# Post-mix and post-FFN norms taken by halves of 288 tokens in an encoder layer

## What is computed

```python
mix = (g_a * (oa @ w_branch_a[i]) + g_b * (ob @ w_branch_b[i])) @ w_out[i]
h = h + rms_norm(mix, g_mix_post[i])
f = jnp.square(jax.nn.relu(rms_norm(h, g_ffn_pre[i]) @ w_up[i])) @ w_down[i]
h = h + rms_norm(f, g_ffn_post[i])
h = h + jax.nn.sigmoid(h @ w_ple_gate[i]) * rms_norm(ple @ w_ple[i], g_ple[i])
```

## Time and profile before

| what | value |
|---|---|
| median of 3 runs | 1178.62 us (1177.7 to 1179.76) |
| the profiled execution | 1179.02 us, span 1177.3 us |
| mean granted TensorE clock | 0.991 |
| TensorE busy | 1151.8 us, 98% of the span |
| VectorE, ScalarE, GpSimd busy | 487.3, 425.9, 508.6 us |

### The profile page before, as it was taken

The page is one execution under the profiler, slowest core; times in us unless marked ns, Lnnn a source line. Parts: engine busy times, 40 slices in busy tenths (PEclk is TensorE's granted clock), DMA queues, the critical chain, the costliest instruction groups (busy, mean ns, idle before and its releaser), DMA issues.

```text
span 1177.3 us, 23187 instructions
## 1 busy us (share of the span) xinstructions
PE 1151.8 (98%) x8374; PEld 1094.8 (93%) x8374; DVE 487.3 (41%) x910; ACT 425.9 (36%) x905; POOL 508.6 (43%) x424
## 2 busy tenths in 40 slices
PE   8999999999999999999999989999999999999897
PEld 7888888888888889999999989999999999999897
DVE  2655555656534341112352276215413421541665
ACT  5344444454443444332233253213212221222342
POOL 3545544453444333333445454534444444444541
PEclk8999999999999999999999999999999999999899
DMA  5233422222232222232222212322222222222122
GB/s 158 82 92 93 137 75 82 89 89 69 84 93 75 92 75 63 81 101 80 81 84 86 63 54 72 99 81 82 87 81 80 80 86 84 80 80 81 53 72 81
DMA packets 167338, 98.82 MB, mean 84 GB/s; under 512 B 8801, under 2 KB 162650, under 8 KB 167282
## 3 DMA queue, kind: packets, MB, share of 16 engines
q1 hardware_dynamic: 159538, 82.05, 24.0%
q0 software_dynamic: 7744, 16.02, 4.2%
HBM read 88.57 MB, written 11.02 MB: 85 GB/s over the span
## 4 chain that ended last, share of the span: by engine, by line
PE 91%; DVE 5%; ACT 1%; issue 1%; POOL 0%; DVEq 0%; ACTq 0%
PE proj L1353 75%; PE turn_out L1525 3%; PE score L1443 3%; PE turn_out L1504 2%; PE turn_out L1520 1%; DVE wide L1219 1%; PE turn_out L1389 1%; PE turn_out L1475 1%; PE score L1450 1%; DVE hT L1248 1%; PE score L1381 1%; ACT prob L679 1%; DVE prob L1043 1%; PE turn_out L1537 1%; DVE act_lo L1237 1%
## 5 line engine op out<-in xcount | busy, mean ns | idle before, releaser
L463 POOL TENSOR_TENSOR w_lo<-w_raw,w_hi 128x512 fp32r<-128x512 f32 x292 | 394.4, 1354 | 587.8 <-ACT w_hi L627 587.6
L1353 PE MATMUL proj<-act_hi,w_hi 128*128 128x288 f32 x1600 | 362.5, 308 | 8.8 <-DVE act_lo L1237 3.5
L1353 PE MATMUL proj<-act_lo,w_hi 128*128 128x288 f32 x1600 | 344.4, 297 | 0.0
L1353 PE MATMUL proj<-act_hi,w_lo 128*128 128x288 f32 x1600 | 343.6, 297 | 0.0
L627 ACT ACTIVATE w_hi<-w_raw 128x512 fp32r<-128x512 f32 x292 | 182.3, 628 | 380.9 <-PE proj L1353 379.2
L1353 PEld LDWEIGHTS proj<-act_hi,w_hi 128*128 128x128 f32 x1600 | 255.0, 190 | 29.8 <-issue 16.6
L1353 PEld LDWEIGHTS proj<-act_lo,w_hi 128*128 128x128 f32 x1600 | 259.0, 190 | 0.0
L1353 PEld LDWEIGHTS proj<-act_hi,w_lo 128*128 128x128 f32 x1600 | 258.8, 190 | 0.0
L1353 PE MATMUL proj<-mid_hi,w_hi 128*128 128x288 f32 x640 | 137.3, 296 | 0.0
L1353 PE MATMUL proj<-mid_hi,w_lo 128*128 128x288 f32 x640 | 137.3, 295 | 0.0
L1353 PE MATMUL proj<-mid_lo,w_hi 128*128 128x288 f32 x640 | 137.3, 295 | 0.0
(11 more groups left out here) (207 smaller groups left out, 1110.7 us busy)
## 6 DMA issues: line engine op xcount, KB each, us to landing
w_raw<-w_in SPq DMA_DIRECT2D x72, 256.0 KB, 3.0
w_raw<-w_up SPq DMA_DIRECT2D x64, 256.0 KB, 2.8
w_raw<-w_down SPq DMA_DIRECT2D x64, 256.0 KB, 2.8
w_raw<-w_gate SPq DMA_DIRECT2D x32, 256.0 KB, 2.7
w_raw<-w_branch_b SPq DMA_DIRECT2D x16, 256.0 KB, 2.9
w_raw<-w_out SPq DMA_DIRECT2D x16, 256.0 KB, 2.8
w_raw<-w_ple_gate SPq DMA_DIRECT2D x16, 256.0 KB, 2.9
out<-k_tm POOLq DMA_DIRECT2D x12, 256.0 KB, 3.8
```

Source lines behind the costliest of these rows:

```text
L463: pool.tensor_tensor(w_lo[:, slot], w_raw[:, slot], w_hi[:, slot].bitcast(F32), ALU.subtract).then_inc(lo_done, 1)
L1353: last = pe.matmul(out[:, h], w[:, slot, at], x[:, k, HALF * h:HALF * h + HALF], start=(k == 0 and s == 0), stop=(k == blocks - 1 and s == 2))
```

## The change

The norms behind `w_out` and behind the last `w_down` group are taken for tokens 0 to 287 and for tokens 288 to 575 apart, each with sums, means, power and row of its own, on 96 partitions by 3 columns.

- TensorE does the last two blocks before the norm half by half: block 6 first half, block 7 first half, block 6 second half, block 7 second half (`last_two`). The sums of the first half stand in the middle of the third of these, its row in the middle of the fourth. The two blocks behind the norm are done for the first half of the tokens over all k, then for the second. Between them and the norm are the four PLE blocks, with the sums of the second half behind the first of them and its row behind the third.
- VectorE, GpSimd and ScalarE do copies, squares, scalings, additions and splits for 288 tokens at a time, first half first. The PLE copies on ScalarE stand between the splits of the first half.
- The pre-FFN norm's sums and row come 4 k-steps later on TensorE than before (`steps_before_sums`), the PLE norm's where they were.
- On ScalarE the eight squares of `ple` stand ahead of the first `gate_ple`.

```diff
-            def behind_norm(half, n, pj, pc):
...
-                project_ple(half, 0)
-                norm_sums(n)
-                project_ple(half, 1)
-                norm_row(n)
-                project_ple(half, 2)
-                project_ple(half, 3)
-                two_tasks(pj, pc, h_split, half * KB)
+            def last_two(n, pj, pc, hi, lo, input_ready):
+                def one(j, h, between):
+                    if h == 0:
+                        wait_projection(Count(pj + j))
+                    for k in range(KB):
+                        p = Count(pc + 2 * j + k // 4)
...
+                        last = half_products(pj + j, p, hi, lo, k, h)
+                        if k == KB // 2 - 1:
+                            between()
...
+                one(0, 0, lambda: None)
+                one(1, 0, lambda: None)
+                one(0, 1, lambda: half_sums(n, 0))
+                one(1, 1, lambda: half_row(n, 0))
             def behind_norm(half, n, pj, pc):
                 project_ple(half, 0)
+                half_sums(n, 1)
                 project_ple(half, 1)
                 project_ple(half, 2)
+                half_row(n, 1)
                 project_ple(half, 3)
+                for h in range(2):
+                    for k in range(KB):
+                        pe.wait_ge(h_split, (2 * half + h) * KB + k + 1)
+                        for j in range(2):
...
+                            half_products(pj + j, p, act_hi, act_lo, k, h)
+            def late_norm(n, pj, pc, steps_before_sums):
                 project(Count(pj + 2), Count(pc + 4), act_hi, act_lo)
-                steps = k_steps(Count(pj + 3), Count(pc + 6), act_hi, act_lo)
-                for _ in range(KB // 2):
+                steps = itertools.chain(k_steps(Count(pj + 3), Count(pc + 6), act_hi, act_lo),
+                                        k_steps(Count(pj + 4), Count(pc + 8), act_hi, act_lo))
+                for k in range(2 * KB):
+                    if k == steps_before_sums:
+                        norm_sums(n)
+                    if k == steps_before_sums + KB // 2:
+                        norm_row(n)
                     next(steps)
...
+            late_norm(N_FPRE, PJ_FF, PC_FF, KB)
...
+            late_norm(N_PLE, PJ_PG, PC_PG, KB // 2)
```

VectorE's update, where `keep` copies a half block out of PSUM and k in BY_VECTOR means the addition is VectorE's:

```diff
+                for k in range(KB - 2, KB):
+                    keep(k, 0)
+                for k in range(KB - 2, KB):
+                    add_square(last_square(2 * n, k, 0), cols=tokens(0))
+                means(2 * n, 0)
+                keep(KB - 2, 1)
+                add_square(last_square(2 * n, KB - 2, 1), cols=tokens(1))
+                dve.wait_ge(row_ready, CHAIN[2 * n] + 1)
+                normed_half(0, 0)
+                normed_half(1, 0)
+                keep(KB - 1, 1)
+                add_square(last_square(2 * n, KB - 1, 1), cols=tokens(1))
+                for k in range(2, KB):
+                    normed_half(k, 0)
+                    rest(k - 2, 0)
+                    if k == 2:
+                        means(2 * n, 1)
+                rest(KB - 2, 0)
+                rest(KB - 1, 0)
+                dve.wait_ge(row_ready, CHAIN[2 * n] + 2)
+                for k in range(KB):
+                    normed_half(k, 1)
+                    if k >= 2:
+                        rest(k - 2, 1)
+                rest(KB - 2, 1)
+                rest(KB - 1, 1)
```

ScalarE, in `next_input` and behind its second call:

```diff
+                for k in range(KB - 2, KB):
+                    square_half(2 * n, x, job, k, 0)
+                for q in range(PC_PLE[n], p):
+                    hi_part(Count(q))
+                square_half(2 * n, x, job, KB - 2, 1)
+                hi_part(Count(p))
+                hi_part(Count(p + 1))
+                square_half(2 * n, x, job, KB - 1, 1)
+                for i in range(KB // 2):
+                    split_hi(i, 0)
+                    keep_ple(n, i)
+                    if i % 2:
+                        hi_part(Count(p + 2 + i // 2))
+                for k in range(KB // 2, KB):
+                    split_hi(k, 0)
+                for k in range(KB):
+                    split_hi(k, 1)
+                    if k >= KB - 2:
+                        hi_part(Count(p + RING + k - (KB - 2)))
...
-            next_input(1, None)
+            next_input(1, down_sum, last_job, None)
+            for k in range(KB):
+                square(SQUARES[N_PLE] + k, ple[:, k])
...
             for m in range(2):
                 gate_ple(m)
                 hi_part(Count(PC_PG + RING + 2 + m))
-            for k in range(KB):
-                square(3 * KB + k, ple[:, k])
```

More of the change, by code:

```diff
@@ L818, in next_input @@
                     else:
-                        act.activation(act_hi[:, k], hT[:, k], ACT.Copy, scale=gcol[:, scale + k:scale + k + 1]
+                        act.activation(act_hi[:, k, c], hT[:, k, c], ACT.Copy, scale=gcol[:, scale + k:scale + k + 1]
                                        ).then_inc(h_hi, 1)
[L822 to L827, removed]
+                for k in range(KB - 2, KB):
+                    square_half(2 * n, x, job, k, 0)
@@ L844, in _ @@
             for k in range(KB):
-                square(KB + k, hT[:, k])
+                square(SQUARES[N_FPRE] + k, hT[:, k])
             for j in range(2, KB):
@@ L1224, in _ @@
+            for m in range(KB - 2):
                 b = (PJ_OUT + m) % 2
@@ L1609, in norm_row, with half_sums @@
             def norm_row(n):
-                pe.wait_ge(r_ready, n + 1)
+                pe.wait_ge(r_ready, CHAIN[n] + 1)
                 row_matmuls(r_t, lambda t: P).then_inc(row_ready, 1)
+            def half_sums(n, h):
+                pe.wait_ge(sq_added, SQUARES[n] + KB + 2 * h)
+                for t in range(3):
+                    first = HALF * h + THIRD * t
+                    last = pe.matmul(turn[0:THIRD, 3 * h + t:3 * h + t + 1], sq_sum[:, first:first + THIRD],
+                                     ones[:, 0:1], start=True, stop=True)
+                last.then_inc(sum_turned, 1)
@@ new lines, in half_row, with half_products @@
+            def half_row(n, h):
+                pe.wait_ge(r_ready, CHAIN[n] + h + 1)
+                for t in range(3):
+                    first = 512 * h + THIRD * t
+                    last = pe.matmul(score[:, first:first + THIRD],
+                                     r_t[0:THIRD, 3 * h + t:3 * h + t + 1].broadcast_to([THIRD, P]),
+                                     ident[0:THIRD, 0:THIRD], start=True, stop=True)
+                last.then_inc(row_ready, 1)
+            def half_products(n, p, hi, lo, k, h):
+                slot, at = p.mod(RING), slice(P * (k % 4), P * (k % 4) + P)
+                for s, (w, x) in enumerate(((w_hi, hi), (w_lo, hi), (w_hi, lo))):
+                    last = pe.matmul(acc[n % 2][:, h], w[:, slot, at], x[:, k, tokens(h)],
+                                     start=(k == 0 and s == 0), stop=(k == KB - 1 and s == 2))
+                if h == 1 and k % 4 == 3:
+                    last.then_inc(w_used, 1)
+                return last
```

239 lines of the change are left out of this document (149 added, 90 removed).

## The result

The changed kernel takes 1182.14 us, median of 15 runs, beside 1178.51 for the kernel before in the same comparison: ratio 1.0031 [1.0024, 1.0039], some 3.7 us slower. The prediction was 1182.7. The profiled execution took 1181.17 us, its span is 1179.6.

The account below looks back on a forecast made before the run. TensorE, busy 98% of the span, loses time waiting for VectorE at two norms. First norm -3.3 + 0.35 + 3.4, second -3.4 + 5.8 + 1.2: +4.05 on 1179.02, 1183.1; median 0.4 lower, 1182.7 us; range 1180 to 1186.

Parts of the forecast that it names:

- VectorE's half chain: First norm: half instructions take 0.45 us; last subtraction ends at u = 26.3, u counted from block 7's old end.
- No wait is there any more: First norm: TensorE reaches the two blocks behind it at u = 10.1, against 15.3, and need not wait.
- the 0.35 that I did count: End of the two blocks behind the first norm: ScalarE's accumulator copy makes TensorE wait 0.35 us more.
- The gains: Stretches around both norms: 3.3 us gained at the first, 3.4 at the second, with VectorE slower than TensorE.
- Given back behind the first norm: Later pre-FFN row returns as waits around the first down block: 1.9 us standing plus 1.5 lower clock, 3.4.
- everything that GpSimd splits there moves with TensorE: Behind the first norm: argument that VectorE's collisions with GpSimd stay, against the later row being absorbed.
- absorbed: Rival, chance 0.18: fewer up-chain collisions with GpSimd remove the later row's 3.4 us; +0.65 left, 1179.3 us.
- Given back behind the second norm: Third gate block: squares ahead of the gate copy make TensorE wait about 5.9 us, then lower clock costs 1.2.
- Costlier halves: Rival, chance 0.10: half instructions on VectorE take 0.53 us, adding 2.9 us in each stretch; 1188.5 us.
- TensorE's pace: Rival, chance 0.12: halves keep pace with TensorE, stretches gain 8.6 and 8.2 us, sum -6.0; 1172.6 us.
- 30.5: First norm: u at which ordinary blocks begin before the change, against 27.2 forecast after it.
- the 3.7 us put to the lower clock: First norm's stretch before the change: 3.7 of 9.0 us lost laid to slow pairs behind two waits.

Follow-up runs that it names:

- the halves' own run: Changed kernel with the PLE squares back behind the second gate copy and the pre-FFN sums and row as early as before: 1172.55 us, ratio 0.9955.
- the run without the additions: Against the halves with squares and pre-FFN row set back: VectorE's six residual additions per norm cut to one column; 1168.98 us, ratio 0.9922.
- filling the gap: Changed kernel plus 42 matmuls with unread results on TensorE before the third gate block: 1179.91 us, ratio 1.0013.
- the whole-block run: Kernel before, whole blocks, with only the eight PLE squares moved ahead of the gate copies: 1181.86 us, ratio 1.0044.

## Why the prediction was right

Point by point, by the prediction's own steps.

- **VectorE's half chain.** A half instruction at 0.45: 0.43 in a chain, as the line of three widths had it. The Trainium skill's page "VectorE: DVE Perf Modes", section on the TRN2 errata, gives 0.457 as an estimate by its formula and advises against such pieces; the rows' 0.43 is near its price, and the halves' own run (0.9955) shows that the advice did not decide here. From the wait-ending addition to the last subtraction I had 22.4 us; it is 22.8 (667.68 to 690.50). Part of that agreement is luck: 36 instructions at 0.43 are 15.5 us where the sum had 16.4, and collisions and waits took some 7.3 where it had 6.0. The addition came at u = 3.6 for 3.9, the wait for the sums was 0.63 for 0.8, VectorE's end u = 26.4 for 26.3.
- **"No wait is there any more" at the two blocks.** One of 0.35 is there, for ScalarE's copy of the last PLE block: the same kind of wait as the 0.35 that I did count at the end of the two blocks. It probably costs nothing by itself, since TensorE catches up with VectorE a few steps on and waits for it there; no run takes it out.
- **The gains**: 3.3 less 0.35 forecast, 2.81 measured; 3.4 forecast, 3.35 measured. The reason given, VectorE as the slower one, is borne out by the waits for `act_lo` and by the run without the additions, in which 2.9 of the 3.6 us taken from VectorE came off.
- **Given back behind the first norm**: 3.4 forecast, 2.05 measured. This is the step of the sum that was mis-sized. The sums came 3.2 us late as reckoned (12.90 us behind the first ordinary block at 704.86, 9.70 before), but the forecast let all of it through, as 1.9 of standing and 1.5 of lower clock, a division that no row gives and that adds up to more than 3.2. VectorE's first `up_t` took up 1.1: 1.87 us before, beside four splits of GpSimd that end at 713.13, 0.76 now, beside three that end at 711.23. That is no chance of phase, as the rival had it, but the split that the change moved ahead of the power: with the row as early as before and this order kept, `up_t` takes 0.81 us too. So "everything that GpSimd splits there moves with TensorE" was the wrong premise, and the rival "absorbed" was a third right. The remaining 2.05 is standing, near the 1.9; the lower clock did not come.
- **Given back behind the second norm**: a wait of 5.9 forecast, 5.97 measured; the lower clock 1.2 forecast, 1.3 measured. Shown by undoing it (-7.1 us), by doing it alone in the kernel before (+5.2), and by filling the gap. (The prediction's own terms, 6.3 + 0.65 - 0.9, make 6.05 and not 5.9.) That TensorE is ready 0.9 behind VectorE holds for half steps alone, as the whole-block run showed.
- **Costlier halves** fell by the 0.43; **TensorE's pace** fell by the waits for `act_lo` that are left (0.95 the longest) and by the run without the additions.
- **Smaller slips.** The "30.5" from which the first gain is taken is 30.63 in the earlier trace rows, the DMA share stands in the earlier trace rows and not in the earlier trace rows, and of the 3.7 us put to the lower clock 3.2 were that.

So the forecast of +4.05 was near since its one large term was right; without it and the later row the sign is the other.

## What to carry to other kernels

Look at an edit's companions: the halves gained 5.3 us by the ratio, and a reordered queue and a later row, which the halves did not need, gave back more than that. An instruction that frees an accumulator should not stand behind a chain whose buffers another engine frees. Where a stall is cut in pieces that each stay short, as here 5.3 us of waits into 3.9, most of the gain can be the clock that no longer falls. And a wait that an experiment removes is worth what the span loses, not what the list of waits loses: 0.8 us in the list were nothing in time.

## What the runs showed of the hardware

- A VectorE subtraction with its operands in SBUF is passed over more than once: it waited through a power and a split (2.18 us) and through two additions and a split (2.63) where it takes 0.51 alone, and with memsets between those it fared no better (2.71). Each time it ends 0.3 us behind the end of a split. The Trainium skill's page "SBUF — State Buffer", section "Who interferes with whom", says that whichever of two such instructions issues first has the ports for the whole instruction. The trace agrees on the collision, and the scaling, whose second input is PSUM, keeps its 0.50 (671.61) beside the same additions. It differs on the order by the starts it records: the split of 670.09 began later than the subtraction of 669.51 and was done before it.
- The loss to the lower clock does not grow with the wait before it: 1.3 us behind 5.97 (clock 0.50 over the next 3.04 us), some 1.7 and 1.5 behind the 1.75 and 2.91 of the earlier trace rows, none behind 1.28 and 0.95. Nor does the wait's length alone decide: behind 1.65 us before the change the clock fell, behind 1.66 us at the same place in the run with the squares first it did not.
